# A four-tap causal convolution moved from VectorE to GpSimd, as products into a temporary and additions

## The reference, cut to what matters

```python
def causal_depthwise_conv(x, w, b):
    s = x.shape[1]
    xp = jnp.pad(x, ((0, 0), (CONV_WIDTH - 1, 0), (0, 0)))
    out = b
    for k in range(CONV_WIDTH):
        out = out + w[k] * xp[:, k:k + s]
    return out

# in hybrid_mixer
z = x @ w_in
a_x, a_gate, q, k, v, f_logit, c_u = jnp.split(z, cuts, axis=-1)
xa = causal_depthwise_conv(a_x, conv_w, conv_b)
out_a = gelu(a_gate) * rg_lru(xa, ...)      # two block-diagonal gates of xa, then a scan over time
out_b = forgetting_attention(...)           # 6 heads of 64, causal, with a forget bias
out_c = s5_ssm(c_u, ...)                    # state-space unit, gelu, gate
o = concatenate([rms_norm(out_a), rms_norm(out_b), rms_norm(out_c)]) @ w_out
```

## Time and profile before

| | |
|---|---|
| runs | 1007.53, 1007.64, 1009.22 us (median 1007.64) |
| profiled execution | 1006.47 us, of which the span is 1004.7 us |
| TensorE busy | 978.8 us (97%) |
| VectorE busy | 669.4 us (67%) |
| ScalarE busy | 528.5 us (53%) |
| GpSimd busy | 256.2 us (26%) |
| TensorE clock granted | full (0.997 as a mean) |
| first mixer stage | about 207 to 326 us; the second one from 494 us later |

### The profile page before, as it was taken

The page is one execution under the profiler, slowest core; times in us unless marked ns, Lnnn a source line. Parts: engine busy times, 40 slices in busy tenths (PEclk is TensorE's granted clock), DMA queues, the critical chain, the costliest instruction groups (busy, mean ns, idle before and its releaser), DMA issues.

```text
span 1004.7 us, 14018 instructions
## 1 busy us (share of the span) xinstructions
PE 978.8 (97%) x5702; PEld 852.9 (85%) x5702; DVE 669.4 (67%) x800; ACT 528.5 (53%) x652; POOL 256.2 (26%) x378
## 2 busy tenths in 40 slices
PE   7999999999899999999999999999998999999997
PEld 6788888899888888888888888888998888888885
DVE  4686755777788756565777775567596886565556
ACT  4554545638882544445546444554688545454551
POOL 3029993010541000000020599900014310000000
PEclk9999999999999999999999999999999999999999
DMA  9755554474135755556495565545732375656551
GB/s 270 262 188 190 187 185 154 145 210 141 71 126 174 221 193 182 195 179 198 134 272 201 178 190 188 170 166 157 201 106 84 126 252 171 206 173 204 171 165 42
DMA packets 142191, 176.47 MB, mean 176 GB/s; under 512 B 11216, under 2 KB 126512, under 8 KB 142128
## 3 DMA queue, kind: packets, MB, share of 16 engines
q1 hardware_dynamic: 140400, 169.30, 53.3%
q0 software_dynamic: 1728, 6.29, 1.9%
HBM read 174.51 MB, written 1.05 MB: 175 GB/s over the span
## 4 chain that ended last, share of the span: by engine, by line
PE 80%; DVE 11%; ACT 2%; SPq 2%; POOL 2%; issue 2%; DMA 1%; DVEq 0%; POOLq 0%
PE bank L1641 29%; PE bank L1643 15%; PE bank L1612 11%; PE bank L1614 10%; PE bank L1613 10%; DVE wlo L1077 2%; SPq L419 2%; PE bank L1617 2%; DMA raw<-in_ffn_w_up 1%; POOL lngb L635 1%; DVE xtok L1297 1%; ACT u L879 1%; DVE xn L1325 1%; DVE xn L1331 1%; DVE xa L1407 1%
## 5 line engine op out<-in xcount | busy, mean ns | idle before, releaser
L1641 PE MATMUL bank<-xT,whi 128*128 128x512 f32 x1280 | 454.3, 399 | 2.4 <-DVE act_lo L1123 1.4
L1077 DVE TENSOR_TENSOR wlo<-raw,whi 128x2048 fp32r<-128x2048 f32 (+1 forms) x157 | 364.4, 2328 | 118.8 <-ACT whi L678 117.9
L1643 PE MATMUL bank<-xT,wlo 128*128 128x256 f32 x1280 | 359.4, 281 | 0.0
L678 ACT ACTIVATE whi<-raw 128x2048 fp32r<-128x2048 f32 (+1 forms) x157 | 297.1, 1897 | 16.5 <-DMA raw<-in_ffn_w_up 6.9
L1641 PEld LDWEIGHTS bank<-xT,whi 128*128 128x128 f32 x1280 | 240.5, 188 | 62.6 <-DVE act_lo L1123 1.7
L1643 PEld LDWEIGHTS bank<-xT,wlo 128*128 128x128 f32 x1280 | 241.8, 189 | 1.2
L1612 PE MATMUL bank<-whi,act_hi 128*128 128x512 f32 x376 | 149.2, 397 | 0.0
L1614 PE MATMUL bank<-whi,act_lo 128*128 128x512 f32 x376 | 147.0, 391 | 0.0
L1613 PE MATMUL bank<-wlo,act_hi 128*128 128x512 f32 x376 | 146.6, 390 | 0.0
L726 ACT ACTIVATE gs<-bank 128x512 f32<-128x512 f32 x40 | 23.9, 598 | 170.9 <-PE bank L1643 170.8
L1117 DVE TENSOR_TENSOR gs<-bank,gs 128x512 f32<-128x512 f32 x40 | 27.6, 691 | 106.4 <-ACT gs L726 106.2
(11 more groups left out here) (315 smaller groups left out, 1259.5 us busy)
## 6 DMA issues: line engine op xcount, KB each, us to landing
raw<-in_ffn_w_up SPq DMA_DIRECT2D x44, 1024.0 KB, 5.4
raw<-in_ffn_w_down SPq DMA_DIRECT2D x44, 1024.0 KB, 5.0
raw<-in_ffn_w_gate SPq DMA_DIRECT2D x43, 1024.0 KB, 5.3
raw<-in_w_in SPq DMA_DIRECT2D x12, 1024.0 KB, 5.3
raw<-in_w_out SPq DMA_DIRECT2D x8, 1024.0 KB, 5.1
raw<-in_w_in SPq DMA_DIRECT2D x12, 512.0 KB, 5.1
lngb<-in_ln_g POOLq DMA_DIRECT2D x6, 512.0 KB, 4.0
lngb<-in_ln_b POOLq DMA_DIRECT2D x6, 512.0 KB, 5.0
```

The source lines that it names most:

```text
L678: A.activation(piece(whi, n, 8, PC)[:, :, cols], piece(raw, n, 8, PC)[:, :, cols], ACT.Copy).then_inc(hi_done, 1)
L1077: V.tensor_tensor(piece(wlo, n, 8, PC)[:, :, cols], piece(raw, n, 8, PC)[:, :, cols], piece(whi, n, 8, PC)[:, :, cols].bitcast(F32), ALU.s ...
L1641: T.matmul(bank[bnk + ft][:, :], hi[:, k, c], xT[:, k, :, :].rearrange("p a n -> p (a n)"), start=k == 0, stop=False)
L1643: ins = T.matmul(bank[bnk + ft][:, 0:SEQ], lo[:, k, c], xT_hi[:, k, :], start=False, stop=k == KD - 1)
```

## The change

`conv(f)` is taken off VectorE and written for GpSimd. GpSimd has each tap as two instructions: a product into a temporary (the free columns of `lngb[:, 0]`) and an addition onto `xa`. It stands ahead of the block moves, behind the one memset of that stage, and a new semaphore `conv_scaled` orders the addition behind the product. ScalarE and TensorE keep their programs.

```diff
--- before.py
+++ after.py
@@ -275,6 +275,7 @@
         u4_ready = sem("u4_ready")
         s_summed = sem("s_summed")
         y_summed = sem("y_summed")
+        conv_scaled = sem("conv_scaled")
         y_gelu = sem("y_gelu")
         half_loaded = sem("half_loaded")
         half_hi = sem("half_hi")
@@ -627,6 +628,19 @@
                 pool.wait_ge(ly.xT_lo_done, 4)
                 pool.memset(qf[:, :, :], 1.0).then_inc(q_ones, 1)
 
+                def conv(f):
+
+                    tap = lngb[:, 0, 3 * SEQ:]
+                    for k in range(1, 4):
+                        if f or k > 1:
+                            pool.wait_ge(ly.conv_step, 3 * f + k - 1)
+                        pool.tensor_scalar(tap, ax[:, f, k:k + SEQ], prow("conv_w", 3 * k + f), 1.0, ALU.mult, ALU.mult)\
+                            .then_inc(conv_scaled, 1)
+                        if k == 1:
+                            pool.wait_ge(ly.conv_first, f + 1)
+                        pool.wait_ge(conv_scaled, 9 * L + 3 * f + k)
+                        pool.tensor_tensor(xa[:, f, :], xa[:, f, :], tap, ALU.add).then_inc(ly.conv_step, 1)
+
                 def attn_scale(h):
 
                     pool.wait_ge(ly.rrec_done, h + 1)
@@ -645,6 +659,10 @@
                         pool.tensor_tensor(squared[g][:, t, :], src(t), src(t), ALU.mult)\
                             .then_inc(ly.o_sq, 1)
 
+                for f in range(3):
+                    pool.wait_ge(ly.z_evac, 5 + f)
+                    conv(f)
+                pool.wait_ge(ly.conv_step, 9)
                 pool.wait_ge(y_gelu, L + 1)
                 for i in (2, 3):
                     block_moves(pool, i)
@@ -1398,15 +1416,6 @@
                 def ahead_mix(m):
                     split_lo(base + MIX_BASE + m + LEAD)
 
-                def conv(f):
-                    for k in range(1, 4):
-                        if k == 1:
-                            vec.wait_ge(ly.conv_first, f + 1)
-                        else:
-                            vec.wait_ge(ly.conv_step, 3 * f + k - 1)
-                        V.scalar_tensor_tensor(xa[:, f, :], ax[:, f, k:k + SEQ], prow("conv_w", 3 * k + f),
-                                               xa[:, f, :], ALU.mult, ALU.add).then_inc(ly.conv_step, 1)
-
                 s5n = [0]
 
                 def s5step(ins):
@@ -1546,13 +1555,10 @@
                 ahead_mix(2)
                 forget_log()
                 forget_series()
-                conv(0)
                 ahead_mix(3)
                 s5_turn_back()
                 s5_scans()
                 s5_turn_on()
-                conv(1)
-                conv(2)
                 ahead_mix(4)
                 ahead_mix(5)
                 attn_logits(0)
```

## The result

The changed kernel takes 1019.0 us (median of four runs, 1018.69 to 1019.73) against 1007.6: a ratio of 1.0113, 95% interval 1.0088 to 1.0137. The forecast was 1010.9 with a range up to 1013.2. The direction was right; the size was 11.4 us where 3.3 were forecast. The profiled execution has a span of 1016.8 us, 12.1 more than before.

A forecast was written before the change was run, and what follows sets the result against it. TensorE, almost without gaps, was taken as the bound, waiting briefly for GpSimd's L635 and VectorE's L1450. Per layer -1.44 + 0.8 + 2.3 = +1.65 us, two layers +3.3, giving 1010.9 us; range 1009.2 to 1012.8, overall 1006.4 to 1013.2.

The forecast's parts named there:

- conv 0 removed, -1.44: First tile's convolution leaves VectorE ahead of the last state-space step: 1.44 us saved per layer.
- its first product and addition hold up the forget operations and the split, +0.8: GpSimd's first convolution instructions delay VectorE's small forget operations and split by 0.8 us per layer, bounds 0 and 1.1.
- Seven meetings from L1443 to L1459, +2.3: VectorE's two-SBUF-input operations meet four additions at 0.42 and three products at 0.2 us: +2.3 per layer, bounds 0 and 4.1.
- L1450 ends near 250.5, TensorE waits 2.1 us, +1.65 per layer: VectorE's last state-space step comes 1.65 us later per layer; TensorE waits about 2.1 us where it waited 0.51.
- All behind it is 1.65 us later.: Everything after TensorE's wait at the state-space output products shifts by 1.65 us per layer, +3.3 us over two layers.
- Conv 1 and 2 off VectorE are worth nothing by itself: Behind the last state-space step, 2.9 us saved before splits and logits gains nothing, as logits need TensorE's score products.
- the 2.88 us are set by ScalarE and the splits: TensorE's 2.88 us idle before the attention-weight transposes comes from ScalarE's chain and the two splits ahead of L635.
- What waits behind GpSimd costs nothing: Block moves behind GpSimd's convolution come 0.5 us late, covered by 1.4 us of slack before the scaling: no cost.
- A: Rival: VectorE is hardly held up; TensorE loses its 0.51 us wait, -0.45 us per layer, 1006.7 us; chance 0.20.
- B: Rival: GpSimd starves until after the splits, delaying gate products and block moves, +1.8 us per layer, 1011.2 us; chance 0.14.
- C: Rival: only four of seven meetings happen, hold-up about 1.4 us cancels the saving, 1007.6 us; chance 0.16.

The follow-up runs named there:

- e1: Changed kernel with eight extra 128x512 matrix products on TensorE where it waits for VectorE's last state-space step: 1011.2 us, ratio 1.0038 to before.
- e2: Kernel before, second tile's convolution kept on VectorE but moved ahead of the scans, nothing new on GpSimd: 1019.0 us, ratio 1.0100.
- e4: Kernel before, VectorE made to wait until GpSimd has scaled the attention weights of heads 0 and 1 before the two splits: 999.1 us, ratio 0.9914.
- e5: Changed kernel with only the first tile's convolution on GpSimd, the second and third on VectorE at their old place: 999.0 us, ratio 0.9913.
- e10: e5 with VectorE's reciprocal of head 0 held back until head 1's exponentials are done: 1010.7 us, ratio 1.0010 to before.
- e11: Changed kernel with VectorE's two splits held back until GpSimd has scaled heads 0 and 1, no extra products: 1011.9 us, ratio 1.0029 to before.
- e9: Changed kernel with four extra products in TensorE's wait in place of eight: 1010.9 us, ratio 1.0021 to before.
- e6: Changed kernel with eight extra products in TensorE's wait and VectorE's splits held back until heads 0 and 1 are scaled: 1002.3 us, ratio 0.9943.
- e8: Kernel before with the second tile's convolution ahead of the scans on VectorE and eight extra products in TensorE's wait: 1007.6 us, ratio 1.0001.
- e3: Changed kernel with GpSimd's 18 products and additions per layer replaced by memsets, leaving out the last three taps: 998.8 us, ratio 0.9909.

## Why the prediction was wrong, point by point

- *conv 0 removed, -1.44; its first product and addition hold up the forget operations and the split, +0.8.* Measured: the split starts at 236.43, 0.46 us ahead of its old 236.89 and, counting the mixer's later start of 0.4, 0.9 ahead. So the two terms together are -0.9 where they were put at -0.6. The first addition did hold up the last forget operation, and the split itself was not lengthened.
- *Seven meetings from L1443 to L1459, +2.3.* Measured, over the durations of the earlier trace rows: 0.13 + 0.58 (the two scans) + 0.09 + 0.54 + 0.16 + 0.53 = 2.0 us. An addition cost 0.5 to 0.6 and a product about 0.1; L1444 met nothing (0.68 us), so there were six meetings, three of them with additions, where seven were reckoned. The mechanism held: alternate turns. Behind the price stood a wrong reading: the "additions" of the earlier trace rows (L645, L580) are products of two tensors. GpSimd's additions of that shape take 0.72 to 0.75 alone (L583 in the earlier trace rows, L642 now), not 0.61.
- *L1450 ends near 250.5, TensorE waits 2.1 us, +1.65 per layer.* It ended at 250.46; the wait is 1.66 us, 1.15 more per layer. The term is right within 0.5 us. That e1 is left with 3.6 us beside the sum of 3.3 is in part luck: 2.4 of them lie at this place.
- *"All behind it is 1.65 us later."* **This is the step that failed.** It took the products behind the wait at their durations of the earlier trace rows, as if a wait cost its own length. They ran at half the clock, for 10.2 and 13.7 us, and took 9.2 us where they took 5.4. I had looked at the granted clock only as a mean over the slices, which reads 9 in every slice before, though the clock had been at half for 3.4 us behind the 2.88 us of waiting, and asked nowhere what a longer idle time would do to it. e1 takes 7.8 us back by keeping TensorE busy, e2 reproduces the loss without GpSimd.
- *"Conv 1 and 2 off VectorE are worth nothing by itself; the 2.88 us are set by ScalarE and the splits."* Wrong, though the result did not show it. The 2.88 us are set by which of two instructions comes first at 261 us, L635 or the first split, and a fraction of a microsecond on VectorE decides it, for 8 to 12 us (e4, e5, e10). In the changed kernel the order stayed the bad one, so this error did not enter the result, but it made me put the chance of a large gain near nothing for edits of this kind.
- *What waits behind GpSimd costs nothing.* Right, but in the changed kernel because the slow clock had made ScalarE late: conv 2 ended at 258.40, 1.1 us behind the forecast, and the block moves waited for ScalarE until 260.73. In e1, with the clock up, they waited for conv 2 (ended 259.24, ScalarE's result was there at 257.54), 1.8 us and not 0.5, and were still done 0.8 us before the reciprocal.
- *Rivals.* A, B and C did not happen. A product did stand aside for a VectorE instruction that followed another without a gap (L637 at 250.07 waited through a whole split), as B's evidence said, but gaps of 0.04 us were enough to let it in.

What stays open is why the clock fell behind a 1.66 us wait in one mixer and not in the other (e11), and behind 0.7 us in e9. The traces show that a filled wait kept it up at the output products in both mixers of e1, e6 and e8. They don't show the condition.

## What to carry to other kernels

Where the busiest engine is a TensorE at full clock, price an added wait at up to its length plus the work behind it at half clock (here 1.2 us of wait and 4 us of clock, mostly but not always paid), and look at the granted clock by stretch, since waits and busy shares don't show it. Before moving work between VectorE and GpSimd, list which VectorE instructions have two SBUF inputs (one with a single input, L1516, was held up too) and which GpSimd instruction is next in line when they run back to back; a short instruction caught behind two long ones can be worth more than the work moved. If it is, an explicit wait that puts the short one first (e4: one line, 9 us) is surer than a timing that happens to let it through (e5, e10).

## What was not expected of the hardware

- When one VectorE instruction follows another without a gap, a GpSimd product (one SBUF tensor in) that waits did not get the turn between them, and an addition did. L637 at 250.07 waited through the rest of L1459 and the 2.28 us split behind it, L635 through 4.6 us of splits; the addition L642 at 245.76 got in between L1455 and L1456, which lasted 1.76 us for 1.22.
- A VectorE instruction with one SBUF input was held up as well. The last forget operation took 0.65 us in place of 0.17 and ended 0.04 us after GpSimd's first addition (235.62 + 0.74 = 236.36); with memsets in GpSimd's place (e3) it took 0.26. Before and after:

```profile
235.24 0.17 DVE L1507 TENSOR_SCALAR logf<-fx 128x12 f32<-128x12 f32 x1
```

```profile
235.62 0.74 POOL L642 TENSOR_TENSOR xa<-xa,lngb 128x256 f32<-128x256 f32 x1
235.75 0.65 DVE L1516 TENSOR_SCALAR logf<-fx 128x12 f32<-128x12 f32 x1
```

- Where the clock fell in a mixer it stayed at half for 3.4, 6.8, 10.2 or 13.7 us, with TensorE busy for most of it.
